# Moving 64 token dots of a PEER layer from the stage over stored blocks to the stage of gate matrices

## What is computed

```python
e = (i1 * PEER_NKEYS + i2).reshape(T, PEER_HEADS * PEER_TOPK)          # 128 experts per token
gate = jax.nn.softmax(cv, axis=-1).reshape(T, PEER_HEADS * PEER_TOPK)
act = jax.nn.gelu(jnp.einsum('ted,td->te', u_tab[e], xb).astype(jnp.float32))
coef = (gate * act).astype(xb.dtype)
return jnp.einsum('te,ted->td', coef, v_tab[e])
```

## Time and profile before

| | before |
|---|---|
| median of 3 runs | 4231.67 us (4220.98 to 4232.37) |
| the profiled execution | 4228.35 us |
| its span, first to last instruction | 4226.7 us |
| busy PE, DVE, POOL, ACT | 89%, 69%, 35%, 25% of the span |
| granted TensorE clock, mean | 0.943 of full speed |
| moved by DMA | 843.15 MB, mean 199 GB/s |

### The profile page before, as it was taken

How to read it: one execution, slowest core, us unless ns; L and a number is a source line. 1 busy time by engine, 2 the same in 40 slices (tenths; PEclk the granted TensorE clock), 3 DMA queues, 4 the chain that set the end, 5 groups by cost and what they waited for, 6 DMA issues and landing times. The chain is left out here.

```text
span 4226.7 us, 60870 instructions
## 1 busy us (share of the span) xinstructions
PE 3779.7 (89%) x21957; PEld 3319.6 (79%) x21957; DVE 2922.2 (69%) x6424; ACT 1052.4 (25%) x1899; POOL 1465.8 (35%) x1174
## 2 busy tenths in 40 slices
PE   4999899888798899999899989998788888889996
PEld 3989788886698899999899989997555655556664
DVE  3653344436311898989799849998788888888776
ACT  4543222224211222222344322221111111111112
POOL 0220244431100000000000025554777777776652
PEclk6999999999899999999999999999899889889998
DMA  4111211214321333333377768888999999999885
GB/s 161 36 41 54 75 51 53 68 31 164 107 90 45 123 117 114 122 110 113 115 195 199 192 224 306 316 305 278 355 380 373 373 373 376 369 372 347 333 332 190
DMA packets 475099, 843.15 MB, mean 199 GB/s; under 512 B 225536, under 2 KB 293376, under 8 KB 473088
## 3 DMA queue, kind: packets, MB, share of 16 engines
q0 software_dynamic: 121680, 447.27, 28.2%
q1 hardware_dynamic: 353200, 393.06, 27.6%
HBM read 718.85 MB, written 121.37 MB: 199 GB/s over the span
## 5 line engine op out<-in xcount | busy, mean ns | idle before, releaser
L2436 PE MATMUL stored_pv<-peer_xh 128*128 128x512 f32 x1200 | 510.6, 426 | 144.8 <-DVE peer_y L2376 128.0
L2376 DVE TENSOR_TENSOR peer_y<-peer_y,stored_pv 128x512 f32<-128x512 f32 x600 | 399.7, 681 | 143.2 <-PE stored_pv L2438 143.1
L2437 PE MATMUL stored_pv<-peer_xl,peer_xh 128*128 128x512 f32 x1200 | 498.0, 415 | 0.0
L2438 PE MATMUL stored_pv<-peer_xh,peer_xl 128*128 128x512 f32 x1200 | 494.0, 412 | 0.0
L2286 POOL DMA_INDIRECT stored_rows<-in_peer_v,peer_idx x384 | 414.0, 1078 | 212.8 <-issue 111.4
L2436 PEld LDWEIGHTS stored_pv<-peer_xh 128*128 128x128 f32 x1200 | 243.6, 203 | 280.7 <-issue 189.6
L1797 PE MATMUL topk_pu<-peer_xh,topk_Uh 128*128 128x384 f32 x1152 | 396.9, 345 | 43.1 <-DVE topk_Ul L1784 43.1
L1798 PE MATMUL topk_pu<-peer_xl,topk_Uh 128*128 128x384 f32 x1152 | 395.2, 343 | 0.0
L1799 PE MATMUL topk_pu<-peer_xh,topk_Ul 128*128 128x384 f32 x1152 | 394.1, 342 | 0.0
L2323 ACT ACTIVATE peer_xh<-stored_Vr 128x1024 fp32r<-128x1024 f32 x100 | 105.0, 1050 | 915.6 <-PE stored_pv L2438 909.1
L2438 PEld LDWEIGHTS stored_pv<-peer_xh,peer_xl 128*128 128x128 f32 x1200 | 242.6, 202 | 56.0
(11 more groups left out here) (372 smaller groups left out, 9147.8 us busy)
## 6 DMA issues: line engine op xcount, KB each, us to landing
stored_Vr<-in_peer_v SPq DMA_DIRECT2D x100, 512.0 KB, 6.6
gates<-gates_G SPq DMA_DIRECT2D x48, 1024.0 KB, 11.2
stored_C<-acts SPq DMA_DIRECT2D x100, 384.0 KB, 6.6
stored_G<-gates SPq DMA_DIRECT2D x100, 384.0 KB, 8.3
topk_Ur<-in_peer_u SPq DMA_DIRECT2D x74, 512.0 KB, 3.5
acts<-topk_act SPq DMA_DIRECT2D x144, 192.0 KB, 1.9
scan_w<-in_w_mod SPq DMA_DIRECT2D x16, 1024.0 KB, 7.2
gates_Ur<-in_peer_u POOLq DMA_DIRECT2D x28, 512.0 KB, 4.6
```

Source lines behind the costliest of these rows:

```text
L2376: nc.vector.tensor_tensor(dst, dst, pv[r % RING][:], ALU.add).then_inc(y_added, 1)
L2436: mm(pv[r % RING][:], Ch[p][j][:, t], Vh[p][j][:, cols], start=(j == 0), stop=False)
L2437: mm(pv[r % RING][:], Ch[p][j][:, t], Vl[p][j][:, cols], start=False, stop=False)
L2438: last = mm(pv[r % RING][:], Cl[p][j][:, t], Vh[p][j][:, cols], start=False, stop=(j == 1))
```

## The change

64 of the 384 dots move from stage_stored to stage_gates. There, after every third bank (192 / 64), VectorE does one dot (L2130 of the changed kernel), and POOL issues the gather of the dot after the next, into two buffers. The rings of `one` and `scaled` shrink from four buffers to two, and VectorE waits for TensorE to be done with the bank before the last (`b + 3` for `b + 1`). The loops of DVE and POOL over the tiles are written out. The indices of the gathers (`idxU`) are turned and converted at the start of stage_gates and no more in stage_experts. Stage_experts does the same number of dots at the same rate, now 64 to 255. Stage_stored has 128 left, four in a step (LATE_RATE 4), again in 32 steps and three buffers. PE's, ACT's and SP's loops stay, but for one load of `row` (512 KB) by SP.

```diff
-EARLY_DOTS, EARLY_RATE, LATE_RATE = 192, 14, 6
+GATE_DOTS, EARLY_DOTS, EARLY_RATE, LATE_RATE = 64, 256, 14, 4
...
-        one = [st.sb(f"one{i}", [P, TG, P]) for i in range(RING)]
-        scaled = [st.sb(f"scaled{i}", [P, TG, P]) for i in range(RING)]
+        one = [st.sb(f"one{i}", [P, TG, P]) for i in range(2)]
+        scaled = [st.sb(f"scaled{i}", [P, TG, P]) for i in range(2)]
+        row = st.sb("row", [P, D])
+        ug = [st.sb(f"ug{i}", [P, D]) for i in range(2)]
+        DOT_EVERY = DENSE * BANKS // GATE_DOTS
...
-            with pool.Fori(0, DENSE) as t:
-                for n in range(A):
-                    ahead.load(pool, t * A + (n + RAWS), n)
+            def u_rows(n):
+                if n >= 2:
+                    pool.wait_ge(dotted, n - 1)
+                pool.indirect_dma_start(ug[n % 2][:], None, dram["peer_u_rows"],
+                                        bass.IndirectOffsetOnAxis(idxU[:, 0, n:n + 1], 0)).then_inc(ug_in[n % 2], 16)
+
+            pool.wait_ge(idx_made, PICKED)
+            for n in range(2):
+                u_rows(n)
+            for t in range(DENSE):
+                for b in range(BANKS):
+                    if b in LOW_AT:
+                        ahead.load(pool, t * A + (LOW_AT.index(b) + RAWS), LOW_AT.index(b))
+                    if dot_after(t, b) and dot_of(t, b) + 2 < GATE_DOTS:
+                        u_rows(dot_of(t, b) + 2)
...
+            def dot(n):
+                dve.wait_ge(ug_in[n % 2], 16 * (n // 2 + 1))
+                nc.vector.scalar_tensor_tensor(out=ug[n % 2][:], in0=ug[n % 2][:], scalar=1.0, in1=row[:], op0=ALU.mult, op1=ALU.mult,
+                                               accum_out=dots[:, 0, n:n + 1]).then_inc(dotted, 1)
+
+            for t in range(DENSE):
                 for b in range(BANKS):
                     if b in LOW_AT:
                         ahead.low(dve, t * A + LOW_AT.index(b), LOW_AT.index(b))
-                    i = b % RING
-                    dve.wait_ge(used, t * BANKS + (b + 1))
+                    i = b % 2
+                    dve.wait_ge(used, t * BANKS + (b + 3))
...
                     last.then_inc(hot, 1)
+                    if dot_after(t, b):
+                        dot(dot_of(t, b))
...
+            sp.dma_start(row[:], dram["rows"][:, 0:D]).then_inc(row_in, 16)
...
-    TASKS, PER = EARLY_DOTS, EARLY_RATE
+    TASKS, PER = EARLY_DOTS - GATE_DOTS, EARLY_RATE
```

More of the change, by code:

```diff
@@ L2047, in _, with stage_gates @@
             turn(TILES - 1)
-def stage_gates(core, xh, xl, picked):
+def stage_gates(core, xh, xl, picked, dots, idxU):
     nc, dram = core.nc, core.dram
@@ L2103, in _ @@
             nc.vector.tensor_copy(picked[:, 0, :], core.slotT[:, 0, 0:FIRST]).then_inc(kept, 1)
-            with dve.Fori(0, DENSE) as t:
+            dve.wait_ge(idx_turned, 1)
+            for g in range(PICKED):
+                nc.vector.tensor_copy(idxU[:, g, :], ahead.pu[0][:, g * P:(g + 1) * P]).then_inc(idx_made, 1)
+            dve.wait_ge(row_in, 16)
+            def dot(n):
[3 more added lines that the diff above has]
+            for t in range(DENSE):
                 for b in range(BANKS):
@@ L2122, in _ @@
             pe.sem_inc(used, RING)
+            pe.wait_ge(kept, 1)
+            for g in range(PICKED):
+                last = nc.tensor.transpose(ahead.pu[0][:, g * P:(g + 1) * P], picked[:, 1, g * P:(g + 1) * P], core.ident[:])
+            last.then_inc(idx_turned, 1)
+            pe.wait_ge(idx_made, PICKED)
             with pe.Fori(0, DENSE) as t:
@@ L2128, in _ @@
                     for j in range(TG):
-                        last = nc.tensor.matmul(pg[i][:, j, :], one[i][:, j, :], scaled[i][:, j, :], start=True, stop=True)
+                        last = nc.tensor.matmul(pg[i][:, j, :], one[b % 2][:, j, :], scaled[b % 2][:, j, :], start=True, stop=True)
                     last.then_inc(used, 1)
@@ L2203, in stage_stored @@
     FROM = EARLY_DOTS // SLOTS
-    row = {g: y[:, g - FROM, :] for g in range(FROM, PICKED)}
-    buffers = [y[:, g, :] for g in range(PICKED - FROM, PICKED)]
+    row = {g: y[:, g, :] for g in range(FROM, PICKED)}
+    buffers = [y[:, FROM - 1, :]]
     buffer = lambda g, j: rows_of[g % VRING][:, j, :]
@@ L2556, in _ @@
         def _(pool):
-            pool.wait_ge(idx_made, PICKED)
             for n in range(TASKS):
@@ L2637, in _ @@
             low_u(1, 1)
[L2638 to L2641, removed]
+            nc.vector.tensor_copy(idx[:], picked[:, 1, :]).then_inc(idx_copied, 1)
             nc.vector.memset(y[:, PICKED:TILES, :], 0.0).then_inc(y_zero, 1)
@@ L2733, in step @@
                     products_u(2 * s + 3, 1)
-            for g in range(PICKED):
-                last = nc.tensor.transpose(pv[0][:, g * P:(g + 1) * P], picked[:, 1, g * P:(g + 1) * P], core.ident[:])
-            last.then_inc(idx_turned, 1)
             run(pe, step)
@@ L2862, in build @@
             core.recycle_semaphores()
+            dots = pr.sb("dots", [P, PICKED, SLOTS])
+            idxU = pr.sb("idxU", [P, PICKED, SLOTS], U32)
             with Stage(core, "retrieve") as rt:
@@ L2865, in build @@
                 stage_topk(core, xh, xl)
-                stage_gates(core, xh, xl, picked)
+                stage_gates(core, xh, xl, picked, dots, idxU)
             y = pr.sb("y", [P, TILES, D])
-            idx, dots = pr.sb("idx", [P, FIRST], U32), pr.sb("dots", [P, PICKED, SLOTS])
-            idxU = pr.sb("idxU", [P, PICKED, SLOTS], U32)
+            idx = pr.sb("idx", [P, FIRST], U32)
             stage_experts(core, xh, xl, y, MADE, picked, idx, dots, idxU)
```

13 lines of the change are left out of this document (8 added, 5 removed).

## The result

| | before | after |
|---|---|---|
| median | 4230.45 us (4220.98 to 4232.37, 4 runs) | 4136.18 us (4132.36 to 4139.24, 4 runs) |
| the profiled execution | 4228.35 us | 4139.24 us |
| its span | 4226.7 us | 4137.6 us |
| granted clock, mean | 0.943 | 0.962 |

The ratio is 0.9781, with a 95% interval of 0.9763 to 0.9799: 94 us less, where 4157 us was forecast, 73 less than the profiled execution. The range, 4118 to 4212 us, held the time.

What follows compares the result with a forecast made beforehand. Bounds: TensorE in the gates stage, DMA in the first 32 stored steps (405 GB/s when full, 2.1 us a step unfed). +48 + 2 - 123 = -73 us on 4228.35 gives 4155, as median 4157 us; range 4118 to 4212.

Steps and rivals of the forecast that it cites:

- Gates, +48 forecast: Gates stage: VectorE becomes the bound with 416 us of work against TensorE's 374, plus ring waits; +48 us (42 to 77).
- the 6 us for the ring: Gates stage: VectorE runs into the two-buffer ring only in pairs of banks without dot or low part; +6 us.
- Gathers in the gates stage: Gates stage: 64 gathers of 512 KB cost nothing while issue and landing fit a cover of 13 us; DMA share about 0.81.
- rival 4: Gates stage: gathers come too late for their dots; at 16 us for issue and landing +175 us, 4280 us; chance 0.08.
- Start of stages: Stage starts: index conversion beside the first `Ur` load, and `row`'s load sharing DMA; +2 us (0 to 4).
- Stored steps, -123 forecast: First 32 stored steps: two gathers and two dots less each, 3.86 us a step saved; -123 us (-85 to -194).
- the step of 22.8 us: Stored stage: new step length with dots, DMA still longest at 22.0 us; bounds 20.6 and 24.0 us.
- POOL's closed loop: Stored stage before: POOL's queue loops through a gather, its landing, the dot and the next gather, 26.3 us in all.
- 1 (feeding stays at 371 GB/s): Stored stage: DMA keeps its average rate, step 24.0 us, gain 85 us, total 4193 us; chance 0.18.
- rival 2: Gates stage: VectorE keeps its waits, perhaps with TensorE at a lower clock; +77 instead of +48, 4184 us; chance 0.10.
- 3 (TensorE's 20.6 us a step): Stored stage: transfers overlap better and TensorE sets the step at full clock, -194 us, total 4084 us; chance 0.05.
- 5: Stored stage: POOL's order and the buffers hold the step, which stays near 26 us; total 4257 us; chance 0.03.

Runs made afterwards that it cites:

- e7: Changed kernel without the 64 dots of the gates stage and their gathers; ring of two and written-out loops kept: 4096.50 us.
- e1: Kernel before, gathers of the 192 stored-stage dots cut to 512 of 1024 columns, dots still over 1024: 4195.74 us, 25.68 us a step.
- e2: Kernel before, the 192 stored-stage dots over 8 columns instead of 1024, gathers whole: 4178.61 us, 25.09 us a step.
- e3: Kernel before with a fourth buffer for gathered u rows in the stored stage: 4188.01 us, 25.44 us a step.
- e5: Changed kernel, the 128 stored-stage dots over 8 columns, gathers whole: 4126.01 us, 22.09 us a step.
- e11: Changed kernel with a fourth buffer for gathered u rows in the stored stage: 4136.55 us, ratio 0.9774, 22.33 us a step.
- e4: Changed kernel, gathers of the 128 stored-stage dots cut to 512 columns, dots still over 1024: 4128.13 us, 22.19 us a step.
- e8: Changed kernel with 96 dots in the gates stage for 64, and 96 left in the stored stage, three a step: 4162.74 us, ratio 0.9848.
- e12: Changed kernel with 16 more dots moved from the stored stage into the whole-block stage: 4162.48 us, ratio 0.9839.
- e6: Changed kernel, the 64 dots of the gates stage over 8 columns, gathers whole: 4097.26 us.
- e10: Kernel before, the 192 stored-stage dots over 8 columns and their gathers over 512: 4137.92 us, 23.73 us a step.

## Why the prediction was right

*Gates, +48 forecast, +44.4 measured.* The pace of a bank (1.63 us) and the dot (1.22 us busy, 1.14 until the next instruction) are as before. Timeline of VectorE in the changed kernel, two banks and a dot, to be read against the earlier trace rows:

```profile
2164.04 0.67 DVE L2140 TENSOR_TENSOR gates_one<-gates_iota,retrieve_slotT 128x512 f32<-128x512 f32 x1
2164.64 1.10 DVE L2143 TENSOR_SCALAR gates_scaled<-gates_iota,retrieve_slotT 128x128 f32<-128x128 f32 x4
2165.67 0.67 DVE L2140 TENSOR_TENSOR gates_one<-gates_iota,retrieve_slotT 128x512 f32<-128x512 f32 x1
2166.27 1.10 DVE L2143 TENSOR_SCALAR gates_scaled<-gates_iota,retrieve_slotT 128x128 f32<-128x128 f32 x4
2167.30 1.21 DVE L2130 SCALAR_TENSOR_TENSOR gates_ug<-gates_ug,gates_row 128x1024 f32<-128x1024 f32 x1
```

In the stage's window of 418.8 us VectorE is busy 412.5 us and waits 5.0 for TensorE. So the 416 us of work were 2 to 3 us too many (a low part was put in with its busy time, 1.23 us, and takes 1.14 from start to start), and the 6 us for the ring are those 5.0. Alone, without the dots, the ring and the loops cost 7.5 us (e7). The forecast had the parts of this term right.

*Gathers in the gates stage, hidden.* Right, and rival 4 with its price fell: they land in 4.4 to 9.2 us, median 6.5, inside the cover of 13. Their issue does not take 5 us beside VectorE's short instructions, but 0.97 to 1.68, as the view of the tile has it (ns, least, median and most):

```profile
L2099 POOL DMA_INDIRECT gates_ug<-in_peer_u_rows,peer_idxU x64: 966/1150/1682, 2044.7 to 2456.7; - x64
```

The DMA share is 0.89, not 0.81, at only 240 GB/s. The sum had put the new bytes in at 405 GB/s, which no window of this stage comes near. The stores of `G` land in 13.6 us for 11.2, and nobody waits for them. The DMA view after:

```profile
gates<-gates_G SPq DMA_DIRECT2D x48, 1024.0 KB, 13.6
...
gates_Ur<-in_peer_u POOLq DMA_DIRECT2D x28, 512.0 KB, 5.1
...
gates_ug<-in_peer_u_rows,peer_idxU POOLq DMA_INDIRECT x64, 6.5
```

*Start of stages, +2 forecast.* The start of the gates stage costs 1.0 us, the hand-over to the stored blocks is 2.4 us shorter, and the rest of the difference, +3.9 us, lies in code that did not change. That last one is spread between executions: over the runs the gates stage begins between 2035.0 us (e1) and 2042.3 (changed).

*Stored steps, -123 forecast, -135.6 measured.* The terms that were mis-sized are the two of the step of 22.8 us: 22.0 us of full transfers at 405 GB/s, and 0.8 unfed. In the run the engines are full all the time (share 1.01, no unfed time), at 396 GB/s over the stage: 8.91 / 396 = 22.5 us, and 22.42 were measured. The 405 of the earlier trace rows were 22 us inside one step, not the level that holds. The two errors, a rate too high and an unfed time that did not come, have opposite signs, and that they leave only 0.4 us a step is luck.

The prediction weighed a rule of the Trainium skill ("DMA: Bandwidth & Descriptors", section "Where 436 GB/s comes from"): the HBM side binds at about 358 GB/s. By it the step would have been an estimated 24.9 us. On this one core e2, e3, e5 and e11 settle at 392 to 401 GB/s, so the measurement decides against it here.

*What was wrong behind the right number.* The prediction said that "DMA is still the longest", with VectorE at 19.8 us and POOL at 19.6 out of the way. e1 and e4 show a second limit less than 1 us beside the first: 25.7 next to 25.1 before, 22.2 next to 22.1 after. Busy time per step did not show it. As I read the waits, it is made of hand-overs: a dot that waits for its gather delays the addition or the low part queued behind it on VectorE, TensorE waits for that, and POOL waits for the dot before it issues the next gather. The prediction did have POOL's closed loop, and a fourth buffer, which opens it, took 1.2 us off the step (e3); how the rest of the second limit is made up is argued from waits, not shown.

One part of it lies inside VectorE's busy time. In the kernel before, one dot and one low part of every step run beside POOL's gate products (3327.68 to 3332.41 us) and take twice their time, 2.3 us for 1.22:

```profile
3328.43 2.27 DVE L2399 SCALAR_TENSOR_TENSOR stored_ug<-stored_ug,peer_y 128x1024 f32<-128x1024 f32 x1
...
3331.23 2.25 DVE L2349 TENSOR_TENSOR peer_xl<-stored_Vr,peer_xh 128x1024 fp32r<-128x1024 f32 x1
```

That is 2.1 us a step before, and 1.8 in the changed kernel, where single dots beside the products take up to 4.8 us. It is part of the 22.1 and 19.8 us that the prediction gives VectorE. No run took it out by itself. TensorE's clock is another rival that no run separates: at 0.89 it is busy 22.7 us a step, at 0.99 20.6, and it may set a part of the second limit before.

That the change lowers both limits at once, by 3.0 us (e2 to e5) and by 3.5 (e1 to e4), is why the forecast held, and it had counted on one of them only. Had the change taken away bytes alone, the same reasoning would have failed: for e1's 1.57 MB a step it gives 1.57 / 405 GB/s = 3.9 us, and e1 got 1.0.

*The rivals.* 1 (feeding stays at 371 GB/s) fell: 396. 2 fell in both of its parts: of VectorE's waits 5.0 us were kept in the gates stage and not 35, and the granted clock stayed at 0.99, with 28 us of new idle time on TensorE. 3 (TensorE's 20.6 us a step) was off by 1.8 us a step. 5 fell with the step.

*What to look for.* Of the signs named, the gates window (418.8 us), VectorE's 98%, the step, its share, its clock and the unchanged late steps came true. VectorE's wait for TensorE, which by more than 10 us would have spoken for rival 2, is 5.0.

No kernel tried that computes the whole layer beats the changed one; with a fourth buffer it is the same within the intervals.

## What to carry to other kernels

Before pricing a stage by its fullest resource, ask for the next limit, and count it with its hand-overs rather than by busy time: here two limits stood within 1 us of each other, and only work that sat in both, a dot with its gather, was worth 2.1 us a piece, while three gathers' worth of bytes alone (e1) or six dots' work on VectorE alone (e2) brought 0.3 us a piece. One more buffer, with no work moved at all, brought 1.2 us a step (e3), some 40 of the 94 us: try that before moving work. Work moved into a stage is free up to the idle time of the engine that takes it and costs its full price from there on: here VectorE got 72 us more to do in the gates stage, its idle time fell from 33.9 to 6.3 us, and the stage became 44.5 us longer; the next 32 dots cost 1.27 us each and brought 0.7. Two neighbouring settings (e8, e12), both some 26 us slower, show how narrow that is: no stage has room left, and each dot cost where it went (1.27 and 1.6 us) more than it brought where it came from (0.7 and 0.6).

## What the runs showed of the hardware

- A DMA share near full does not mean that bytes are moving fast, nor that the stage is held by it. In the gates stage of e6 it is 0.96 at 263 GB/s, and its products take 1.5 us more than without the gathers (e7: 0.66, 178 GB/s); in the stored stage 1.01 goes with 396. Even within the stored stage the ratio of rate to share differs by window: 327 / 0.88 = 372 GB/s in the late steps before, 328 / 0.85 = 386 in e1, 396 / 1.01 = 392 in the changed kernel.
- Two-operand instructions of VectorE over 1024 columns that run beside POOL's products of 128x768 take 2.3 us for 1.22 (before), and single ones up to 4.8 us (changed). Additions that read PSUM (0.68 us) keep their time beside the same products.
- The granted clock over the stored steps, a mean over stretches at 2.4 and at 1.2 GHz: 0.89 with 15% of TensorE's time idle (before), 0.93 to 0.95 with 13 to 14% (e1 to e3), 0.99 with 8% (changed), but also 0.98 with 12% idle in e10. Its busy time per step fell from 22.7 (before) to 20.6 us (changed) for the same instructions.
